# Latent attention: the value products of a finished pair of heads, issued before or after the next unit's transposes and scores

## What is computed

```python
MLA_HEADS, MLA_NOPE, MLA_ROPE, MLA_V, Q_BLOCK, SEQ = 8, 64, 32, 64, 128, 512

def block(args):                       # one block of 128 queries
    qn, qr = args
    s = (jnp.einsum('bqhd,bkhd->bhqk', qn, k_nope)
         + jnp.einsum('bqhr,bkr->bhqk', qr, k_rope))
    p = jax.nn.softmax(s.astype(jnp.float32) * scale, axis=-1).astype(v.dtype)
    return jnp.einsum('bhqk,bkhd->bqhd', p, v)

o = lax.map(block, (qn_b, qr_b))       # four blocks
```

## Time and profile before

| | us |
|---|---|
| median of 3 runs | 1036.38 |
| lowest and highest of them | 1036.14, 1036.41 |
| the profiled execution, its own time | 1036.81 |
| its span in the trace | 1035.1 |
| latent attention, first scores to last values | 210.7 to 295.4 |
| PE busy over the span | 1018.1 (98%) |
| DVE, ACT, POOL busy over the span | 579.1, 409.2, 220.3 |

### The profile page before, as it was taken

One profiled execution on the slowest core, in us unless ns is written; L12 is line 12 of the kernel. 1 busy time (PEld: TensorE's weight loads), 2 busy tenths in 40 slices (PEclk: granted clock), 3 DMA queues, 4 the chain that ended last, 5 costly groups with the idle time before them and its releaser, 6 DMA issues.

```text
span 1035.1 us, 14399 instructions
## 1 busy us (share of the span) xinstructions
PE 1018.1 (98%) x5792; PEld 847.9 (82%) x5792; DVE 579.1 (56%) x771; ACT 409.2 (40%) x592; POOL 220.3 (21%) x293
## 2 busy tenths in 40 slices
PE   8999999999999999999999999999999999999996
PEld 7889898866678999888888888888888888888884
DVE  6785447577767889555151525443333324367786
ACT  6545555665433212633232323442222212235656
POOL 4010000635763331000000001003442223302002
PEclk9999999999999999999999999999999999999998
DMA  9422240000100014244543538527678772336562
GB/s 295 153 82 81 63 131 2 1 2 11 16 17 1 2 43 123 61 134 161 165 162 133 178 133 266 127 82 178 137 179 169 164 174 83 110 112 206 163 187 108
DMA packets 110642, 118.91 MB, mean 115 GB/s; under 512 B 13349, under 2 KB 91633, under 8 KB 110320
## 3 DMA queue, kind: packets, MB, share of 16 engines
q1 hardware_dynamic: 102528, 90.45, 28.9%
q0 software_dynamic: 7888, 27.47, 10.7%
q10 hardware_dynamic: 160, 0.07, 0.0%
HBM read 115.36 MB, written 25.69 MB: 136 GB/s over the span
## 4 chain that ended last, share of the span: by engine, by line
PE 95%; DVE 2%; ACT 1%; issue 1%; DMA 0%; DVEq 0%; ACTq 0%
PE psum L1017 24%; PE psum L1018 24%; PE psum L1019 24%; PE psum L1345 2%; PE psum L1320 2%; PE psum L1352 2%; PE psum L1365 1%; PE psum L1444 1%; PE psum L1502 1%; PE psum L1490 1%; PE psum L1417 1%; PE psum L1456 1%; PE psum L1165 1%; PE psum L1306 1%; PE psum L1186 1%
## 5 line engine op out<-in xcount | busy, mean ns | idle before, releaser
L1017 PE MATMUL psum<-hT_hi,w_hi 128*128 128x512 f32 x704 | 274.8, 390 | 0.5 <-DVE hT_lo L2256 0.5
L1019 PE MATMUL psum<-hT_hi,w_lo 128*128 128x512 f32 x704 | 274.0, 389 | 0.0
L1018 PE MATMUL psum<-hT_lo,w_hi 128*128 128x512 f32 x704 | 273.9, 389 | 0.0
L2206 DVE TENSOR_TENSOR w_lo<-w_raw,w_hi 128x2048 fp32r<-128x2048 f32 (+3 forms) x69 | 143.1, 2074 | 148.5 <-ACT w_hi L1703 148.5
L1703 ACT ACTIVATE w_hi<-w_raw 128x2048 fp32r<-128x2048 f32 (+3 forms) x70 | 119.7, 1711 | 139.2 <-PE psum L1019 125.7
L1017 PEld LDWEIGHTS psum<-hT_hi,w_hi 128*128 128x128 f32 x704 | 132.2, 188 | 28.1 <-issue 0.7
L1019 PEld LDWEIGHTS psum<-hT_hi,w_lo 128*128 128x128 f32 x704 | 132.2, 188 | 27.6
L1018 PEld LDWEIGHTS psum<-hT_lo,w_hi 128*128 128x128 f32 x704 | 132.2, 188 | 26.9
L2206 DVE TENSOR_TENSOR acts<-gate_act,psum 128x512 f32<-128x512 f32 x22 | 15.1, 687 | 99.6 <-PE psum L1019 98.4
L1017 PE MATMUL psum<-w_hi,a_hi 128*128 128x512 f32 x154 | 60.2, 391 | 0.2
L1018 PE MATMUL psum<-w_lo,a_hi 128*128 128x512 f32 x154 | 59.9, 389 | 0.0
(11 more groups left out here) (337 smaller groups left out, 1800.9 us busy)
## 6 DMA issues: line engine op xcount, KB each, us to landing
w_sum<-in_ffn_w_down_dram POOLq DMA_DIRECT2D x32, 704.0 KB, 6.8
w_raw<-in_ffn_w_gate_up_dram SPq DMA_DIRECT2D x44, 512.0 KB
w_raw<-in_w_in_dram SPq DMA_DIRECT2D x21, 1024.0 KB
dw<-w_sum SPq DMA_DIRECT2D x22, 512.0 KB, 4.5
dw<-in_ffn_w_down_dram SPq DMA_DIRECT2D x33, 256.0 KB, 3.0
w_raw<-in_w_out_dram SPq DMA_DIRECT2D x4, 1024.0 KB
x_tok<-in_x_dram SPq DMA_DIRECT2D x4, 512.0 KB, 5.2
w_raw<-in_mem_w_kv_dram SPq DMA_DIRECT2D x2, 1024.0 KB
```

The source lines that it names most:

```text
L1017: pe.matmul(o, s_hi, m_hi, start=first, stop=False)
L1018: pe.matmul(o, s_hi, m_lo, start=False, stop=False)
L1019: return pe.matmul(o, s_lo, m_hi, start=False, stop=last)
L2206: return dve.tensor_tensor(o, a, b, op)
```

## The change

In the loop on PE, the call of `latent_values(n - 2)` moves from behind `latent_scores(n + 2)` to ahead of `latent_turn(n)`, in every even unit from 2 to 30.

```diff
             for n in range(NT * H):
+                if n > 0 and n % 2 == 0:
+                    latent_values(n - 2)
                 latent_turn(n)
                 if n + 2 < NT * H:
                     latent_scores(n + 2)
-                if n > 0 and n % 2 == 0:
-                    latent_values(n - 2)
                 if n % H == 2 and n > H:
                     spread_sums(n // H - 1)
                 beside_attention(n)
```

## The result

| | before | after |
|---|---|---|
| median us (7 runs each) | 1036.28 | 1039.54 |
| lowest, highest | 1036.12, 1036.84 | 1039.32, 1040.27 |
| profiled execution, its own time | 1036.81 | 1039.41 |
| its span | 1035.1 | 1037.7 |
| turn(0) to L1400 in the trace | 214.02 to 295.36: 81.34 | 213.50 to 297.94: 84.44 |

The changed kernel is slower, at a ratio of 1.0031 with a 95% interval of 1.0022 to 1.0041. The medians are 3.26 us apart, against 3.03 in the prediction's sum. In the traces the attention has grown by 3.10 us, and what lies behind L1400 has kept its length (1035.1 - 295.36 = 739.74 us before, 1037.7 - 297.94 = 739.76 after). The spans differ by 2.6 only, because the attention happened to begin 0.52 us earlier in the profiled execution of the changed kernel; over the traces of this study turn(0) starts between 213.36 and 214.02.

The account below looks back on a forecast made before the run. PE's queue was taken to set the time in the attention and behind it. Waits for the copy of 2.43 us plus 0.60 for neighbours on the array gave 3.03, so 1036.38 + 3.0 = 1039.4 us, range 1036.9 to 1041.2.

Parts of the forecast that it names:

- Units 24 and 26: Values wait for a copy standing behind a row maximum, starting 2.50 behind scores(e): 0.24 us each, 0.48 in all.
- Unit 22: Values wait for copy(21), which stands behind the two `dec_lo` multiplications: 0.76 us, the largest wait.
- Units 8, 12 and 18: Copy behind a decay's subtraction or `dec_lo`, with only a short decay (L1306) beside the scores: 0.21 us each, 0.63.
- Unit 30 and the end: Late copies behind DVE's division delay values(28) and values(30) at the attention's end: cost 0.56 us.
- Units taken at nothing: Units 2, 4, 6, 10, 14, 16, 20 and 28: the copy is hidden, so no wait.
- Changes of shape: PE switching between all-column and half-column products: net five more changes at 0.12 us each, 0.60 in all.
- Values directly behind L1306 or L1320: Eight units, no row showing it; taken at no extra cost, bounds for five of them -0.75 to +0.45 us.
- The bounds: Hand-over at 0 or 0.25 in eight waits (-1.2, +0.8), plus -0.75 or +0.45: added cost 1.1 to 4.3 us.
- The rival of the copies in time: Waits of 0.24 and 0.21 vanish in the attention; about 0.9 us slower, 1037.3 us; chance 0.21.
- The rival of a gain: Later turns no longer wait for `p_tok`, exponentials rather than copies come last: 0.8 us gained, 1035.6 us; chance 0.05.
- The rival of a bound DVE: DVE's queue eats the turns' slack, so seven units taken at no wait also wait: another 3.5 us, 1042.9; chance 0.08.
- part two: Cost on PE of which product shapes are neighbours on the array: 0.60 us of the 3.03.

Follow-up runs that it names:

- values_between: Against the kernel before, the values stand between turn(n) and scores(n+2) in all fifteen units; 1040.86 us, +4.48 us by the medians.
- spread_first: The kernel before, with the spread of the sums issued ahead of the values in units 10, 18 and 26; 1035.14 us, 1.22 us under before.

## Why the prediction was right

The forecast was 1039.4 us, and 1039.54 was measured. The mechanism was the one forecast: values that wait for their copy, and changes of shape. Term by term, in the trace of the changed kernel:

- Units 24 and 26, 0.24 each: measured 0.24 and 0.24 (scores to values 1.20 for 0.96). The start 2.50 behind scores(e) was met to 0.01.
- Unit 22, 0.76: measured 0.76.
- Units 8, 12 and 18, 0.21 each: the decay L1306 to the values takes 0.72, 0.73 and 0.72, where decay to turn took 0.51 or 0.52. Met.
- Unit 30 and the end, 0.56: values(28) are 2.83 behind scores(30) (2.86 forecast) and values(30) 5.98 (6.01). From turn(29) to L1400 the changed kernel lost 0.48, so this term reads 0.08 too large. 0.03 of it is the start of the values. The other 0.05 is a matter of where the cut is laid: turn(29) took 0.49 to its scores before and 0.44 now, and the same 0.05 comes back in unit 22, where turn(22) takes 0.49 for 0.44 because values now stand ahead of it.
- Units taken at nothing: right for 2, 4, 6, 10, 14, 16 and 20. In unit 28 the values waited 0.09 (1.04 behind scores(29)), and the wait of turn(28) for its exponential, which before made 0.95 of 0.86, went; the two cancelled. The prediction had neither: it read that scores to turn is 0.87 with a wait and without one, which turn(28) contradicts.
- Changes of shape, 0.60: the trace gives 0.15 in unit 4, 0.16 in unit 10, 0.14 in unit 14, 0.14 beyond the wait in unit 18, 0.24 in unit 26 and 0.15 less in unit 8, in all 0.68. The term was right to 0.1. Its unit price was not general: 0.12 each in unit 26, 0.14 to 0.16 for single changes in this order, and 0.20 in `values_between`.
- Values directly behind L1306 or L1320, taken at no extra cost with no row to show it: 0.43 and 1.09, the same as a turn in that place. The choice by the nearest row held.

With the measured terms in place the sum is 0.48 + 0.76 + 0.63 + 0.48 + 0.68 = 3.03, against 3.10 by the lengths; 0.04 of the rest is in unit 22 (turn(21) to turn(23) grew by 0.80). That this is the forecast's own 3.03 is luck: the end was 0.08 under its term and the shapes 0.08 over. The bounds were drawn a little too wide, since the hand-over to values(30) stands in the time of before too, and so counts in seven waits and not in eight (1.05 down and 0.7 up).

The rival of the copies in time is refuted by all nine waits of the changed kernel, in which the values start 0.14 or 0.15 behind the end of the copy, and by the two orders with a doubled copy. The rival of a gain is refuted by late turns that gained nothing: most of the p_tok waits ahead of later turns are a matter of the load queue. PE time were those of turn(28), 0.14 as `spread_first` shows, and of turn(31), 1.23 behind values(28) for 1.03; neither made the changed kernel faster, because in unit 28 a wait for the copy and the turn behind the values took the time back, and at the end the copies come last. The rival of a bound DVE did not come true in the changed kernel, but its mechanism exists: with DVE's queue 0.7 us longer, or with one value group fewer between scores and turn, the exponential becomes the last to come.

The Trainium skill, TensorEngine Tiling (Array Packing), section Key Properties, says that a change of tiling mode drains TensorE and a change of tile alone does not. That agrees with part two, 0.6 of the 3.0, whose price came from the rows; the kernels with full columns show the pause going with the shape, and no run shows the drain itself. The Trainium skill, VectorE: DVE Perf Modes, section The DRAIN you can't avoid, says that the next operation waits for the empty pipe, which by the prediction's estimate would have added 0.4. The same section says that a next operation that is not held back starts earlier, which the prediction did not use; the changed kernel's trace shows the copy starting 0.61 behind a row maximum of 0.69 (278.93 to 279.54), and the sum without the 0.4 fits.

## What to carry to other kernels

Before a consumer is moved up in an engine's queue, lay the new sequence over a place of the old trace where the same instructions already stand in that order; the distance from the producer's end to the consumer's earliest start, less what stays between them, is the cost, unit by unit. Here PE is busy for 97% of the stretch (83.42 of 86.00 us), and each wait cost nearly its full length, and each pause that was filled gave nearly its full length back. And count what an order keeps apart: here one value group stood between each scores product and its turn, and moving it by one place too few cost more than moving it the whole way (4.26 us for 3.10).

## What the runs showed of the hardware

- From the end of DVE's copy, as recorded, to the start of the PE products that waited for it: 0.14 or 0.15 us in every place: once in the kernel before (values(30)), nine times in the changed kernel (units 8, 12, 18, 22, 24, 26, 28, 30 and the end), and fourteen times with the doubled copy in the changed order.
- Going from products on all columns to products on half of them and back costs PE 0.24 us when a transpose follows (0.09 to enter, 0.09 to leave and 0.06 in the transposes) and more when a 512-column product follows (scores to the next group 1.06 for 0.95). A value group of four products on all columns takes 0.89 to the next transposes, one of eight on half of them 1.02.
- On DVE the doubled copies start 0.72 us apart where one waits for the other (279.88 to 280.60), and 0.60 apart where a copy and a row maximum do not depend on each other (275.12 to 275.72).
